# Five of eight row pairs of a feed-forward layer through seven block products, and down projections added to X by DMA

## What is computed

```python
hf = rms_norm_2(x, g_ffn[layer])
x = x + (jax.nn.silu(hf @ w_gate[layer]) * (hf @ w_up[layer])) @ w_down[layer]
return rms_norm_2(x, g_final)
```

## Time and profile before

| | |
|---|---|
| Time, median of 3 runs | 2486.65 us (2486.57 to 2486.88) |
| Profiled execution: time | 2486.79 us |
| Profiled execution: span | 2485.0 us |
| TensorE busy | 2472.1 us (99%) |
| VectorE busy | 1771.4 us (71%) |
| ScalarE busy | 1276.0 us (51%) |
| GpSimd busy | 192.0 us (8%) |
| Nine turns | from about 1882 to 2454 us |

### The profile page before, as it was taken

The page is one execution under the profiler, slowest core; times in us unless marked ns, Lnnn a source line. Parts: engine busy times, 40 slices in busy tenths (PEclk is TensorE's granted clock), DMA queues, the critical chain, the costliest instruction groups (busy, mean ns, idle before and its releaser), DMA issues.

```text
span 2485.0 us, 28892 instructions
## 1 busy us (share of the span) xinstructions
PE 2472.1 (99%) x10962; PEld 2036.7 (82%) x10962; DVE 1771.4 (71%) x2253; ACT 1276.0 (51%) x1619; POOL 192.0 (8%) x319
## 2 busy tenths in 40 slices
PE   9999999999999999999999999999999999999998
PEld 7888788888888888888888889888888888888887
DVE  6665665665675666675666866776678899988897
ACT  6454444444555444444545556566555555555554
POOL 0010000000011000010001100010100000000000
PEclk9999999999999999999999999999999999999999
DMA  9667666666688777776778754667766666666664
GB/s 333 208 223 221 208 212 211 204 218 202 210 241 259 231 233 223 226 234 210 228 238 262 235 180 149 233 203 220 229 211 220 220 217 212 210 211 218 218 210 148
DMA packets 263610, 545.31 MB, mean 219 GB/s; under 512 B 14768, under 2 KB 21040, under 8 KB 263088
## 3 DMA queue, kind: packets, MB, share of 16 engines
q1 hardware_dynamic: 242304, 477.39, 59.3%
q0 software_dynamic: 21168, 66.08, 9.5%
HBM read 508.29 MB, written 35.13 MB: 219 GB/s over the span
## 4 chain that ended last, share of the span: by engine, by line
PE 92%; DVE 5%; issue 2%; ACT 0%; DMA 0%; POOL 0%; DVEq 0%; ACTq 0%
PE job L2266 25%; PE job L2267 25%; PE job L2272 25%; DVE lo L2060 1%; PE group L2693 1%; PE group L2692 1%; PE group L2702 1%; PE att L2702 1%; PE att L2692 1%; PE att L2693 1%; PE job L2643 1%; PE job L2644 1%; PE job L2645 1%; DVE X L1343 1%; PE att L2643 1%
## 5 line engine op out<-in xcount | busy, mean ns | idle before, releaser
L1287 DVE TENSOR_TENSOR lo<-raw,hi 128x1024 fp32r<-128x1024 f32 (+1 forms) x736 | 879.2, 1213 | 504.8 <-ACT hi L729 483.9
L729 ACT ACTIVATE hi<-raw 128x1024 fp32r<-128x1024 f32 (+1 forms) x736 | 768.9, 1054 | 867.1 <-PE job L2272 808.9
L2266 PE MATMUL job<-hi,xh 128*128 128x512 f32 (+1 forms) x1696 | 663.0, 391 | 0.3 <-ACT hi L729 0.3
L2267 PE MATMUL job<-hi,xl 128*128 128x512 f32 (+1 forms) x1696 | 657.2, 388 | 0.0
L2272 PE MATMUL job<-lo,xh 128*128 128x512 f32 (+1 forms) x1696 | 451.0, 388 | 0.0
L2266 PEld LDWEIGHTS job<-hi,xh 128*128 128x128 f32 x1696 | 318.5, 188 | 68.5 <-issue 2.4
L2267 PEld LDWEIGHTS job<-hi,xl 128*128 128x128 f32 x1696 | 318.5, 188 | 66.4 <-issue 2.1
L2272 PEld LDWEIGHTS job<-lo,xh 128*128 128x128 f32 x1696 | 317.3, 188 | 65.1
L2266 PE MATMUL job<-hi,ah 128*128 128x512 f32 x832 | 325.9, 392 | 0.0
L2267 PE MATMUL job<-hi,al 128*128 128x512 f32 x832 | 323.8, 389 | 0.0
L2272 PE MATMUL job<-lo,ah 128*128 128x512 f32 x832 | 222.5, 389 | 0.0
(11 more groups left out here) (409 smaller groups left out, 2534.5 us busy)
## 6 DMA issues: line engine op xcount, KB each, us to landing
raw<-in_ret_w_in SPq DMA_DIRECT2D x94, 1024.0 KB, 5.2
raw<-in_pool_w_in SPq DMA_DIRECT2D x64, 1024.0 KB, 5.6
raw<-in_w_down SPq DMA_DIRECT2D x44, 1024.0 KB, 5.2
raw<-in_w_gate SPq DMA_DIRECT2D x72, 512.0 KB, 3.9
raw<-in_w_up SPq DMA_DIRECT2D x72, 512.0 KB, 4.8
raw<-in_ret_w_out SPq DMA_DIRECT2D x32, 1024.0 KB, 5.3
raw<-in_pool_w_out SPq DMA_DIRECT2D x32, 1024.0 KB, 5.3
raw<-in_w_in SPq DMA_DIRECT2D x28, 1024.0 KB, 6.0
```

The costliest lines, as they stand in the source:

```text
L729: act.activation(hi[:, (U.at * 2 + h) % HS, :, 0:n], src, ACT.Copy).then_inc(hi_ready, 1)
L1287: dve.tensor_tensor(lo[:, (U.at * 2 + h) % LS, :, 0:n], src, hi[:, (U.at * 2 + h) % HS, :, 0:n].bitcast(F32), ALU.subtract).then_inc(lo_re ...
L2266: pe.matmul(o, oh[:, kt, ts], w, start=first and k == 0, stop=False)
L2267: pe.matmul(o, ol[:, kt, ts], w, start=False, stop=False)
```

## The change

It changes `BILINEAR` from (0, 2, 4, 6) to (0, 2, 3, 5, 6), moves the tiles of the weight sums by 32 bytes, gives the token sums of the fifth pair the places of `krT` and `qrp`, and makes the down projections of the nine turns go to X in another way: ScalarE copies them to two buffers in the place of `gfb`, and GpSimd adds these to X with DMAs, one after the other. `gfb` is then loaded after the last add. In block units BANK5 goes before BANK3. Low part 1 of a block unit's sums goes, where another block unit follows, between that unit's first `lo` and its third sum.

```diff
-BILINEAR = (0, 2, 4, 6)
+BILINEAR = (0, 2, 3, 5, 6)
...
-            ("fblk", [P, TT, 4, 4 * BK]), ("fT", [P, TT * 4, 4 * BK]),
+            ("fblk", [P, TT, 4, 4 * BK]), ("fT", [P, TT * 4, 4 * BK]), ("even", [P, 8]),
...
+        drawn = [gfb[:, 2 * NB * n:2 * NB * (n + 1)].rearrange("p (t n) -> p t n", t=TT) for n in range(2)]
...
+        def down_at(i, j):
+
+            return 4 * (i - PAIRED) + j
...
+        TOKENS = [v for v in range(KV) if v != BILINEAR[-1]] + [BILINEAR[-1]]
...
@@ sync
-                if u == 1:
-                    sp.wait_ge(half_used, 2 * FU)
-                    sp.dma_start(gfb[:, :], g_final.rearrange("(a n) -> a n", a=1).broadcast_to([P, D])).then_inc(gf_in, 16)
...
+            sp.wait_ge(down_added, 16 * DOWN_ADDS)
+            sp.dma_start(gfb[:, :], g_final.rearrange("(a n) -> a n", a=1).broadcast_to([P, D])).then_inc(gf_in, 16)
@@ gpsimd
-            for i in range(FC):
+            def add_down(i, j):
+
+                n = down_at(i, j)
+                pool.wait_ge(down_copied, n + 1)
+                if n:
+                    pool.wait_ge(down_added, 16 * n)
+                pool.dma_start(X[:, :, NB * j:NB * (j + 1)], drawn[n % 2], accum_op=ALU.add).then_inc(down_added, 16)
+
+            for i in range(PAIRED):
                 turn_across(NF + i, fblk[:, :, :, :], fT[:, :, :])
+            wait_drained(pool, ffn_at(PAIRED)[1] - 1)
+            for i in range(PAIRED, FC):
+                if i > PAIRED:
+                    turn_across(NF + i - 1, fblk[:, :, :, :], fT[:, :, :])
+                for j in range(3 if i == FC - 1 else 4):
+                    add_down(i, j)
+            turn_across(NF + FC - 1, fblk[:, :, :, :], fT[:, :, :])
+            add_down(FC - 1, 3)
@@ scalar
+            def copy_down(i, j):
+
+                U, J, _ = ffn_at(i)
+                n = down_at(i, j)
+                wait_job(act, U + (KV + 1 + j))
+                if n >= 2:
+                    act.wait_ge(down_added, 16 * (n - 1))
+                for t in range(TT):
+                    ins = act.activation(drawn[n % 2][:, t, :], pair[(J + j) % 2][t][:, :], ACT.Copy)
+                ins.then_inc(down_copied, 1)
...
                     pair_high(U + v, i, v, 0)
+                    if v == 0 and i > PAIRED:
+                        copy_down(i - 1, 2)
+                    if v == 1 and i > PAIRED:
+                        copy_down(i - 1, 3)
                     if v - 1 in BILINEAR:
                         high_sums(i, v - 1, 1)
...
-                    if v == 6:
+                    if v == 4:
                         hidden_high(I, ah)
...
                 split_hi(U + 1)
-                if i < FC - 1:
-                    split_hi(U + 2)
                 act.wait_ge(gate_made, nth(i))
...
-                if i == FC - 1:
-                    split_hi(U + 2)
+                split_hi(U + 2)
+                copy_down(i, 0)
                 split_hi(U + 3)
+                copy_down(i, 1)
...
+            copy_down(FC - 1, 2)
             kept_hi(0)
+            copy_down(FC - 1, 3)
@@ vector
                 if n:
-                    dve.wait_ge(sums_low, 2 * n)
+                    dve.wait_ge(sums_low, 2 * n - 1)
...
                 low_of(U, 0, slice(0, 2))
+                if v - 1 in BILINEAR:
+                    low_sums(i, v - 1, 1)
                 if v:
                     sum_two(U, i, v)
...
-                        if v == 1:
+                        if v == 1 and i == PAIRED:
                             accumulate(J - 1, U, 3)
...
-                    if v == 6:
+                    if v == 4:
                         hidden_low(I, al, ah)
...
-                accumulate(J, U + 1, 0)
                 split_lo(U + 2)
-                accumulate(J + 1, U + 2, 1)
                 split_lo(U + 3)
                 start_next(U + 4, i + 1)
-                accumulate(J + 2, U + 3, 2)
...
                 dve.wait_ge(half_done, 4 * t + c + 1)
+                if t == 0 and c in (0, 3):
+                    dve.wait_ge(down_added, 16 * (DOWN_ADDS - 1 if c == 0 else DOWN_ADDS))
...
-            accumulate(Pos(DOWN_J - 1), Pos(DOWN_U), 3)
@@ tensor
+            def down_bank_free(i, j):
+
+                if i < PAIRED:
+                    wait_drained(pe, ffn_at(i)[1] + j)
+                else:
+                    pe.wait_ge(down_copied, down_at(i, j) + 1)
...
-                    wait_drained(pe, J - 2)
+                    down_bank_free(i - 1, 2)
...
+                pe.wait_ge(sums_low, 2 * n + 1)
+                product(BANK5[:, :], s_high[:, 1], s_low[:, 1], wsh[:, 0], wsl[:, 0], opens, closes)
                 wait_pair(U, 1)
-                product(BANK3[:, :], sh[:, s, 3], sl[:, s, 3], hi[:, b, 1], lo[:, b, 1], opens, closes).then_inc(half_used, 1)
-                pe.wait_ge(sums_low, 2 * n + 1)
-                product(BANK5[:, :], sh[:, s, 1], sl[:, s, 1], wsh[:, 0], wsl[:, 0], opens, closes)
+                product(BANK3[:, :], s_high[:, 3], s_low[:, 3], hi[:, b, 1], lo[:, b, 1], opens, closes).then_inc(half_used, 1)
                 if first:
-                    wait_drained(pe, J - 1)
+                    down_bank_free(i - 1, 3)
```

More of the change, by code:

```diff
@@ L271, in build @@
         x_blk[3] = xL[3][0].rearrange("p (t q) c -> p t q c", q=4)
-        sg, fg, gfb, fblk, fT, wsums, wsh, wsl, p1s, u2 = stage(
+        sg, fg, gfb, fblk, fT, _, wsums, wsh, wsl, p1s, u2 = stage(
             ("sg", [P, TT, NB]), ("fg", [P, TT, NB]), ("gfb", [P, D]),
-            ("fblk", [P, TT, 4, 4 * BK]), ("fT", [P, TT * 4, 4 * BK]),
+            ("fblk", [P, TT, 4, 4 * BK]), ("fT", [P, TT * 4, 4 * BK]), ("even", [P, 8]),
             ("wsums", [P, 4, NB]), ("wsh", [P, 4, NB], F32R), ("wsl", [P, 4, NB], F32R),
@@ L321, in build @@
         first_copied, seventh_read = sem("first_copied"), sem("seventh_read")
+        down_copied, down_added = sem("down_copied"), sem("down_added")
         gate_made, gate_ready, up_made = sem("gate_made"), sem("gate_ready"), sem("up_made")
@@ L410, in four, with combined @@
             return raw[:, U % RAW].rearrange("p a b n -> p (a b) n")
+        TOKENS = [v for v in range(KV) if v != BILINEAR[-1]] + [BILINEAR[-1]]
+        def combined(s, high):
+            if s < 4:
+                return (sh if high else sl)[:, s]
+            return (sh_last if high else sl_last)[:, :, :]
         def difference(v, high):
@@ L1992, in tokens_made, with tokens_low @@
                     dve.tensor_tensor(x_sums[:, 0:2], first, second, ALU.subtract).then_inc(tok_made, 1)
[L1994 to L1996 removed]
+            def tokens_low(at):
+                v = TOKENS[at]
+                dve.wait_ge(tok_high, at + 1)
                 if v in BILINEAR:
                     n = BILINEAR.index(v)
[L1999 removed]
+                    dst, high, srcs = combined(n, False), combined(n, True), x_sums
                 else:
@@ L2250, in _, with unit @@
         def _(pe):
-            def unit(U, J, oh, ol, k0, start=False, stop=False, n=NB, groups=None, filled=group_done, halves=(0, 1)):
-                if start and not (J.i is None and J.at < 2):
+            def unit(U, J, oh, ol, k0, start=False, stop=False, n=NB, groups=None, filled=group_done, halves=(0, 1), free=False):
+                if start and not free and not (J.i is None and J.at < 2):
                     pe.wait_ge(drained[J % 2], (J // 2).value())
@@ L2665, in bilinear_unit @@
                 product(BANK2[:, :], xh[:, k + 1, one], xl[:, k + 1, one], hi[:, a, 1], lo[:, a, 1], opens, closes).then_inc(half_used, 1)
+                pe.wait_ge(sums_low, 2 * n + 1)
+                product(BANK5[:, :], s_high[:, 1], s_low[:, 1], wsh[:, 0], wsl[:, 0], opens, closes)
                 wait_pair(U, 1)
-                product(BANK3[:, :], sh[:, s, 3], sl[:, s, 3], hi[:, b, 1], lo[:, b, 1], opens, closes).then_inc(half_used, 1)
-                pe.wait_ge(sums_low, 2 * n + 1)
-                product(BANK5[:, :], sh[:, s, 1], sl[:, s, 1], wsh[:, 0], wsl[:, 0], opens, closes)
+                product(BANK3[:, :], s_high[:, 3], s_low[:, 3], hi[:, b, 1], lo[:, b, 1], opens, closes).then_inc(half_used, 1)
                 if first:
-                    wait_drained(pe, J - 1)
-                product(BANK7[:, :], sh[:, s, 0], sl[:, s, 0], wsh[:, 1], wsl[:, 1], first, last).then_inc(sums_used, 1)
+                    down_bank_free(i - 1, 3)
+                product(BANK7[:, :], s_high[:, 0], s_low[:, 0], wsh[:, 1], wsl[:, 1], first, last).then_inc(sums_used, 1)
                 pe.wait_ge(sums_low, 2 * n + 2)
-                ins = product(BANK6[:, :], sh[:, s, 2], sl[:, s, 2], wsh[:, 2], wsl[:, 2], first, last)
+                ins = product(BANK6[:, :], s_high[:, 2], s_low[:, 2], wsh[:, 2], wsl[:, 2], first, last)
                 if last:
@@ L2734, in ffn_turn @@
                         pe.wait_ge(seventh_read, nth(i))
-                    unit(U + j, J + j, ah, al, 0, start=True, stop=True)
+                    if j >= 2:
```

(2 more changed lines are left out.)

23 lines of the change are left out of this document (15 added, 8 removed).

## The result

The change makes the kernel slower: 2542.81 us (2542.62 to 2543.61, 5 runs) against 2486.65 (2486.41 to 2487.69, 5 runs), a ratio of 1.0226 [1.0214, 1.0237] (in square brackets the 95% interval), or 56.2 us more. The forecast was 2521.1, 34.4 more, in a range of 2506 to 2562. So the sign and the bound were right, and the size was 22 short. In the profiled execution the span is 2541.5, at a granted clock of 0.996.

What follows compares the result with a forecast made beforehand. VectorE's packed stretch was taken as the bound: eight turns at 2.67 (21.3) plus 13.1 in the tail, 34.4 on the profiled 2486.79, gave 2521.2, or 2521.1 as median; own range 2511 to 2537, wider range 2506 to 2562.

Steps and rivals of the forecast that it cites:

- The bound: VectorE's order of work inside a turn, not its total, sets the pace; a turn gets 2.67 us longer, 21.3 in eight.
- packed stretch: VectorE's gapless work from unit 0's low second sums to unit 6's, said to grow from 29.62 to 33.69 us.
- Rival B: Whole kernel faster: TensorE's 11.6 us are saved and only the tail stalls lightly, 2475 to 2481; chance 0.05.
- The first turn: First of nine turns: no hidden layer (2.67) in it, keeps its accumulate, stretch of 31.0 us, so no change.
- The adds: Four 512 KB adding DMAs a turn on GpSimd's queue, one at a time, said to cost the turns nothing.
- D: Time of one adding DMA to landing: taken as 5 us, with nothing lost up to 6.8.
- Rival A: Adds slower than 6.8 us delay ScalarE's copies and the hidden layer: 7 a turn, 56 in all, 2577; chance 0.2.
- Covered by 1.0: The hidden layer's transposition arrives at 19.2 us into a turn, 1.0 before its read in unit 4 at 20.2.
- The tail: After the last turn: transposition queued behind the third add, TensorE waits 11.1 us, plus 2 for its clock: 13.1.
- the low clock: TensorE resumes at 1.2 GHz after the tail's wait, costing 2 us; bounds nothing and 10.9.
- The alignment: The 32-byte shift speeds TensorE's products on the weight sums: between nothing and 0.4 us a turn.
- rival D: The 32-byte shift does nothing: no change to the forecast, only 0.03 us a turn touched; no chance given.

Runs made afterwards that it cites:

- e6: The kernel after the change, with ScalarE's copy of the fourth down projection moved behind the high second sums and the next split: 2572.20 us, ratio 1.0356.

## Why the prediction was right, and what it mis-sized

**The bound.** Right, and shown. The packed stretch of VectorE, not its total, sets the turn. Five pairs with VectorE's accumulates give +2.5 a turn where 2.67 stood, copies added give 66.6 where 66.25 stood, and another order in the stretch gives nothing. TensorE's waits before each B6 are where they were forecast. Rival B, with the saved matmuls paying, would have needed turns near 62.3; no five-pair kernel came under 65.1.

**The first turn**, taken as unchanged, grew by 2.2 (62.96 to 65.15). The step "its stretch is 31.0, it stays where it was" failed: the stretch runs from 1884.42 to 1917.80, 33.4. VectorE waits in it for the shared `wsh`, 1.60 here:

```profile
1897.78 1.23 DVE L2121 TENSOR_TENSOR wsl<-wsums,wsh 128x1024 fp32r<-128x1024 f32 x1 [1.60 <-ACT wsh L1238]
```

**Later turns without adds**: 66.6 for 66.25, 0.35 a turn, 3 us in eight. The stretch lasts 34.33 (2149.78 to 2184.11 in the run without adds) where 33.69 + 0.3 stood: in units 3 and 6 the step behind the low second sums starts 1.31 and 1.32 after them and not 1.14.

**The adds.** The mis-sized term was D. I took 5 from issue to landing, nearest to the 3.4 of a plain transfer, and set the limit at 6.8. The first two of a turn together take from 2139.50 to about 2154.4, 15 or 7.5 each (8.7 and 5.6 to landing), so the copy of the fourth projection starts at t = 1.21 where 0.26 was forecast. Rival A's mechanism is therefore real, past its own limit, but at D near 7.5 it is worth 1.4 a turn on average (68.06 against 66.64) and not A's 7. Add four goes out at t = 8.4 (forecast 2.3), the write behind it needs 6.3, and the hidden layer is there at 22.6, not at 19.2. "Covered by 1.0" was the weakest statement: ScalarE already waits 1.11 there, and with four pairs or an earlier VectorE this wait is the bound. Over nine turns the adds cost 37.7 - 26.3 = 11.4, where I had nothing.

The Trainium skill, "Collectives: The Full Stack", section "The bandwidth ceiling", puts a reducing DMA at about half a copy's rate, for its second source read. This case bears it out in part at most: the first add of a turn takes 8.7 where a plain transfer takes 6.0, less than twice as long, and at a turn's second place the add is no slower. With the Trainium skill's "DMA: Bandwidth & Descriptors", anatomy of one DMA, the estimate for 1 MB read was 4.4, lower than any add measured, 5.0 at least.

**The tail.** The mechanism was right, the issue time wrong: the third add went out at 2494.71 = E + 2.4, not E - 3.6, because its predecessors were late too. The transposition's write followed at E + 3.1, where E - 2.9 stood; from it to TensorE took 13.6, against 14.26 before. So TensorE waited 16.72 for 11.1, and the low clock cost 2.2 for 2. That term was near by luck: the time for which the clock stays low differs from kernel to kernel (last section), and no row stood for it. The wait of `mh` behind the last copy, 3.4 by itself, was missed.

**The alignment.** 0.4 a turn stood in TensorE's saving. It isn't there; as rival D said, that moves nothing, since VectorE sets B6.

In sum the turns were 37.7 for 21.3 (first turn 2.2, slower turns 3, adds 11.4) and the tail 18.9 for 13.1. The forecast's own range, 2511 to 2537, doesn't hold the 2542.8; the wider one does, by the part that was added for slow adds, and slow adds are what came.

**Open.** Why the return of the hidden layer comes at t = 23.4 to 27.2 when VectorE is early and at 21.6 to 24.9 when it is late. The write doesn't differ: with the fourth copy behind (e6) and in the kernel after it is issued at t = 8.9 to 10.7, and its read follows 6 to 9 later. From the read's issue to ScalarE it takes 7.1 to 9.9 with the fourth copy behind, and 5.2 to 7.3 in the kernel after (9.5 to 10.8 with four pairs). So the read back differs. More weight loads beside it would be a reason, but no run shows that. Nor was a second buffer for the sums tried, which might let VectorE use an earlier start.

## What to carry to other kernels

Before leaving out work on the busiest engine, find the stretch of the second engine that must be done by a fixed point, and count only what the edit adds to and takes from that stretch: the change took four accumulates a turn from VectorE and gained nothing by it, while one at the stretch's head was worth 5 us in the kernel before. A transfer that is given to a queue delays what is queued behind it; give it a place where no one waits, and order the queue again for the last turn, where nothing follows to cover it. When a read moves to an earlier unit, price its producer's whole way through the queue, and treat a cover of 1 us in 20 as none.

## What was not expected of the hardware

- An accumulating DMA of 512 KB from SBUF to SBUF takes hardly longer than a plain one at the median (5.9 and 5.8), but the first of a turn takes 8.5 to 9.5 against 5.8 to 7.1, and with one add a turn each takes 8.6 to 10.6. It holds GpSimd for 1.19 rather than 0.72.
- `across<-fblk`, also 512 KB, lands in 3.4 alone on its queue, in 5.7 to 7.5 right behind an add in the kernel after, and in 5.2 to 6.9 right behind a plain transfer; in the last turn of the tail's reordering it took 9.6.
- A stop of 3.38 was enough for TensorE's clock to fall. Windows of the kernel without adds, in which TensorE had stopped at 2480.79:

```profile
2482.00:2484.00 2.00, 0.00 (x0) 0.72 0.58 120
2484.00:2486.00 2.00, 1.83 (x4) 0.50 0.96 397
...
2490.00:2492.00 2.00, 2.00 (x10) 1.00 0.02 4
```

It starts again at 2484.17 at 1.2 GHz and has 2.4 GHz only after 2489. The stall of 3.4 in the tail so costs 5.5. In the eleven kernels that stop before the tail, for 3.38 to 17.30, the matmuls that follow run at the lower level for 1.9 to 6.1, which costs 0.9 to 2.4. The time doesn't go with the length of the stop: 1.9 stood behind 17.30, 6.1 behind 4.71.
